# A hybrid trunk step on one core: gated branch products kept in their banks, and the mixed chunk rounded by ScalarE

## What is computed

```python
br = jnp.stack([a_out, b_out, c_out, d_out], axis=2)
gates = jax.nn.sigmoid(gpre.reshape(B, S, N_BRANCH, D_MODEL))
mixed = jnp.sum(gates * jnp.einsum('bsnc,ncd->bsnd', br, p['w_branch']), axis=2)
x = x + gate1 * (mixed @ p['w_out'])
h2 = rms_norm(x, p['norm2_w']) * (1 + scale2) + shift2
x = x + gate2 * expert_choice_ffn(h2, p['w_router'], p['w_gate'], p['w_up'], p['w_down'])
```

## Time and profile before

| | |
|---|---|
| median of three runs | 2066.54 us |
| profiled execution | 2068.15 us (span of its trace 2066.4 us) |
| PE busy | 1793.6 us, 87% |
| DVE busy | 645.3 us, 31% |
| ACT busy | 548.3 us, 27% |
| POOL busy | 518.7 us, 25% |
| mean granted clock of TensorE | 0.95 |
| chain that ended last | PE 49%, DMA 33%, DVE 9%, POOL 4%, ACT 3% |

### The profile page before, as it was taken

How to read it: one execution, slowest core, us unless ns; L and a number is a source line. 1 busy time by engine, 2 the same in 40 slices (tenths; PEclk the granted TensorE clock), 3 DMA queues, 4 the chain that set the end, 5 groups by cost and what they waited for, 6 DMA issues and landing times.

```text
span 2066.4 us, 22539 instructions
## 1 busy us (share of the span) xinstructions
PE 1793.6 (87%) x9096; PEld 1138.6 (55%) x9096; DVE 645.3 (31%) x1349; ACT 548.3 (27%) x1054; POOL 518.7 (25%) x654
## 2 busy tenths in 40 slices
PE   5989999999899788878879899999996987888787
PEld 2878897789553222222248788967882422222223
DVE  2185245647310001001144642556653000000111
ACT  3433343222431111101144333522224211110111
POOL 0785343148200000000037652523561000000000
PEclk8999898999999999999989998989998999999999
DMA  9524533455589999999973253335544999999996
GB/s 350 138 102 138 181 105 117 175 165 207 207 360 426 426 427 426 428 426 427 427 210 123 79 206 111 113 138 172 194 177 170 389 427 428 426 428 426 427 426 265
DMA packets 123543, 567.76 MB, mean 275 GB/s; under 512 B 21808, under 2 KB 31280, under 8 KB 98352
## 3 DMA queue, kind: packets, MB, share of 16 engines
q1 hardware_dynamic: 112656, 543.91, 66.5%
q10 hardware_dynamic: 9920, 20.84, 2.8%
q0 software_dynamic: 864, 1.58, 0.3%
HBM read 550.57 MB, written 15.73 MB: 274 GB/s over the span
## 4 chain that ended last, share of the span: by engine, by line
PE 49%; DMA 33%; DVE 9%; POOL 4%; ACT 3%; issue 1%; SPq 1%; ACTq 0%; DVEq 0%
PE banks L769 22%; PE banks L1269 11%; DMA ring<-in_w_up 9%; DMA ring<-in_w_gate 7%; DMA ring<-in_w_down 6%; DMA work<-in_w_gate 4%; POOL ring_fp32r L710 3%; DMA work<-in_w_up 3%; PE banks L775 2%; DMA ring<-in_w_ada 2%; DVE work L1845 2%; DMA work<-in_w_down 1%; PE banks L1086 1%; PE banks L1065 1%; ACT work L1368 1%; PE banks L1239 1%
## 5 line engine op out<-in xcount | busy, mean ns | idle before, releaser
L710 POOL TENSOR_TENSOR ring_fp32r<-ring,ring_fp32r 128x256 fp32r<-128x256 f32 x592 | 467.2, 822 | 912.4 <-ACT ring_fp32r L1368 911.9
L1269 PE MATMUL banks<-ring,work 128*64 128x512 f32 x1776 | 402.6, 597 | 74.9 <-DMA ring<-in_w_gate 33.3
L769 PE MATMUL banks<-xT_fp32r,ring_fp32r 128*128 128x384 f32 x1280 | 356.0, 351 | 1.6 <-POOL ring_fp32r L710 1.6
L1368 ACT ACTIVATE work<-banks 32x512 f32<-32x512 f32 (+7 forms) x404 | 205.7, 528 | 487.3 <-PE banks L1269 250.8
L1269 PEld LDWEIGHTS banks<-ring,work 128*64 128x64 f32 x1776 | 122.4, 136 | 333.2 <-issue 198.8
L1269 PE MATMUL banks<-work 128*64 128x512 f32 x972 | 225.8, 601 | 42.8 <-DMA work<-in_w_gate 15.1
L769 PEld LDWEIGHTS banks<-xT_fp32r,ring_fp32r 128*128 128x128 f32 x1280 | 241.3, 195 | 10.6 <-issue 3.6
L769 PE MATMUL banks<-hT_fp32r,ring_fp32r 128*128 128x384 f32 x640 | 219.4, 343 | 0.0
L1368 ACT ACTIVATE ring_fp32r<-ring 128x1024 fp32r<-128x1024 f32 (+1 forms) x164 | 154.8, 970 | 158.2 <-PE banks L769 126.8
L2247 DVE SCALAR_TENSOR_TENSOR xT<-banks,mod,xT 128x128 f32<-128x128 f32 (+1 forms) x128 | 47.0, 413 | 446.3 <-PE banks L1305 446.0
L1269 PEld LDWEIGHTS banks<-work 128*64 128x64 f32 x972 | 67.7, 137 | 182.9 <-issue 112.4
(11 more groups left out here) (287 smaller groups left out, 1687.3 us busy)
## 6 DMA issues: line engine op xcount, KB each, us to landing
ring<-in_w_up SPq DMA_DIRECT2D x38, 2048.0 KB, 30.6
ring<-in_w_gate SPq DMA_DIRECT2D x37, 2048.0 KB, 30.5
ring<-in_w_down SPq DMA_DIRECT2D x36, 2048.0 KB, 30.3
ring<-in_w_in SPq DMA_DIRECT2D x28, 2048.0 KB, 8.4
ring<-in_w_ada SPq DMA_DIRECT2D x24, 2048.0 KB, 8.5
work<-in_w_down SPq DMA_DIRECT2D x20, 2048.0 KB, 30.6
work<-in_w_gate SPq DMA_DIRECT2D x18, 2048.0 KB, 30.5
work<-in_w_up SPq DMA_DIRECT2D x16, 2048.0 KB, 30.6
```

The lines of the kernel that those rows point to most:

```text
L710: ins = pool.tensor_tensor(rounded(w_), w_, rounded(hi_), ALU.subtract)
L769: mm = pe.matmul(dst, a_, b_, start=(first and i == 0), stop=(last and i == 2))
L1269: mm = pe.matmul(dst[64 * hf:64 * hf + 64, :], x(k), w[kk][:, 512 * hf:512 * hf + 512], start=(k == 0), stop=(k == KC - 1), tile_position= ...
L1368: return act.activation(dst, src, ACT.Copy, scale=scale)
```

## The change

In VectorE's loop the products of banks b and b + 1 are written back into these banks (one instruction of 768 columns); those of banks b + 2 and b + 3 go to TMPB. Three sums of 384 columns follow, each with one operand in a bank and one in TMPB: bank b plus TMPB 0 into bank b; bank b + 1 plus TMPB 1 into TMPB 1; bank b plus TMPB 1 into MIX. The last of them counts up `bp_evac`, so the banks are released at the end of a chunk and not after its products. The cast leaves VectorE.

ScalarE gets a loop over the eight chunks: it rounds weight quarter `Q_BRANCH + dc + 4`, waits for `bp_evac` of chunk dc, writes the rounded chunk MIXH, counts up `mix_ready`, and for the first four chunks issues the gate load of chunk dc + 4. GpSimd's, TensorE's and SP's code is the same.

```diff
--- before.py
+++ after.py
@@ -1608,17 +1608,18 @@
 
                 for slot in spilled:
                     act.wait_ge(slot, 16 * (SPILLED // 8) * (l + 1))
-                for dc in range(8):
+                for dc in range(4):
                     if dc == 0:
                         act.wait_ge(sem["br_ready"], l + 1)
                     if dc == 2:
                         act.wait_ge(sem["tokens_free"], l + 1)
-                    if dc >= 4:
-                        high_parts(Q_BRANCH + dc + 1)
-                        act.wait_ge(sem["mix_ready"], 8 * l + dc - 3)
                     act.dma_start(GT[dc % 4], spill[l, dc]).then_inc(gate_in[dc % 4], 16)
-                for dc in range(4, 8):
+                for dc in range(8):
                     high_parts(Q_BRANCH + dc + 5)
+                    act.wait_ge(sem["bp_evac"], 8 * l + dc + 1)
+                    copy(rounded(MIXH[:, dc, :]), MIX[:, dc, :]).then_inc(sem["mix_ready"], 1)
+                    if dc < 4:
+                        act.dma_start(GT[dc], spill[l, dc + 4]).then_inc(gate_in[dc], 16)
                 for k in range(KC):
                     if k < 4:
                         high_parts(Q_OUT + k + 5)
@@ -2187,15 +2188,15 @@
                     dve.wait_ge(sem["bp_out"], 8 * l + dc + 1)
                     dve.wait_ge(gate_in[dc % 4], 16 * (2 * l + dc // 4 + 1))
                     b = 4 * (dc % 2)
-                    STT(TMPB[:, 0:3, :], GT[dc % 4], 1.0, PS[:, b:b + 3, 0:T], ALU.add, ALU.mult)
-                    STT(TMPB[:, 3, :], GATES[:, dc, :], 1.0, PS[:, b + 3, 0:T], ALU.add, ALU.mult).then_inc(sem["bp_evac"], 1)
+                    STT(PS[:, b:b + 2, 0:T], GT[dc % 4][:, 0:2, :], 1.0, PS[:, b:b + 2, 0:T], ALU.add, ALU.mult)
+                    STT(TMPB[:, 0, :], GT[dc % 4][:, 2, :], 1.0, PS[:, b + 2, 0:T], ALU.add, ALU.mult)
+                    STT(TMPB[:, 1, :], GATES[:, dc, :], 1.0, PS[:, b + 3, 0:T], ALU.add, ALU.mult).then_inc(dve_step, 1)
+                    dve.wait_ge(dve_step, step())
+                    TTo(PS[:, b, 0:T], PS[:, b, 0:T], TMPB[:, 0, :], ALU.add)
+                    TTo(TMPB[:, 1, :], PS[:, b + 1, 0:T], TMPB[:, 1, :], ALU.add).then_inc(dve_step, 1)
+                    dve.wait_ge(dve_step, step())
+                    TTo(MIX[:, dc, :], PS[:, b, 0:T], TMPB[:, 1, :], ALU.add).then_inc(sem["bp_evac"], 1)
                     dve.wait_ge(sem["bp_evac"], 8 * l + dc + 1)
-                    TTo(TMPB[:, 0:2, :], TMPB[:, 0:2, :], TMPB[:, 2:4, :], ALU.add).then_inc(dve_step, 1)
-                    dve.wait_ge(dve_step, step())
-                    TTo(MIX[:, dc, :], TMPB[:, 0, :], TMPB[:, 1, :], ALU.add).then_inc(dve_step, 1)
-                    dve.wait_ge(dve_step, step())
-                    dve.tensor_copy(rounded(MIXH[:, dc, :]), MIX[:, dc, :]).then_inc(sem["mix_ready"], 1)
-                    dve.wait_ge(sem["mix_ready"], 8 * l + dc + 1)
                 for dc in range(8):
                     if dc == 0:
                         dve.wait_ge(sem["x_moved"], 32 * (l + 1))
```

## The result

The changed kernel took 2047.42 us (median of 7 runs, 2039.8 to 2053.39), the kernel before, run beside it, 2058.64 us (7 runs). The ratio is 0.9933, 95% interval 0.9907 to 0.9959: faster by 0.67%. The interval reaches past 0.995, so whether the gain is over the half percent that the prediction set as its bound isn't decided. Over all repeated runs of this study the two means are 2061.4 us (66 runs of before) and 2049.4 us (25 of after), 12.1 us apart with a standard error of 1.2. The forecast was 8.6 us less and 2057.9 us, with a range down to 2048.0. The result is 0.6 us under that range.

The account below looks back on a forecast made before the run. VectorE and GpSimd, taking turns in the branch sums, were held to share the bound. TensorE's lost times there, 4.3 us a layer, gave 2 x 4.3 = 8.6 us off the median 2066.54: 2057.9 us, range 2048 to 2067.

Parts of the forecast that it names:

- The bound: In the branch sums of each layer: GpSimd carries the chain at 4.97 us a round, VectorE is as full.
- GpSimd's piece of 0.72 us: One 128x256 weight subtraction on GpSimd (L710): 0.72 us without turns with VectorE, against 1.54 beside an SBUF-to-SBUF sum.
- TensorE without a stop: Branch matmuls and first 48 of the output projection in one group, no wait on VectorE or GpSimd: 4.3 us a layer.
- The break-even for a late release: In the branch sums: banks freed at chunk end; at 4.8 us a VectorE chunk the output projection starts as before.
- A: VectorE's bank writes cost double: 4.75 us a chunk, gain 0.4 to 0.6 us a layer, about 2065.5; chance 0.10.
- C: Slower: banks come free late in the branch sums; at 5.6 us a chunk 11 us lost, about 2078; chance 0.05.
- B: GpSimd's pieces don't get faster: 5.0 us a chunk, TensorE resumes at 508 as before, 2066.5; chance 0.08.
- D: Layer 1's gain is swallowed by the expert weight stream; one layer's 4.3 us remains, 2062.2; chance 0.07.
- the start of the sum: The level for the whole program: median of before, 2066.54 us, from three runs spanning 2056.85 to 2066.82.
- the later stages wait on this chain, so I pass the gain on in full: Stages behind the branch sums in both layers start earlier by the whole gain, 2 x 4.3 = 8.6 us.
- The term of the sum: Gain from the first branch matmul to the output projection's first pair: 4.3 us a layer, 8.6 us in all.
- 0.62 for the same: Whole program: chance of a time within half a percent, 10.3 us (2056.2 to 2076.9), of the kernel before.

Follow-up runs that it names:

- the control: The changed kernel with one more 128x384 product on VectorE a chunk, one operand in a bank; first branch matmul to pair's end 45.01 and 45.26 us.

## Why the prediction was right or wrong

**Right.** The bound: GpSimd and VectorE share it and slow each other (the kernel with only the cast moved, the extra subtraction, and the two added products). VectorE's chunk of 3.54 us: measured 3.54. The bank-to-bank product of 951 ns: 963; the sum in its bank of 545: 566. GpSimd's piece of 0.72 us: 0.738 in the median, with gaps. TensorE without a stop: one group, 4.46 and 4.62 us gained for 4.3. The break-even for a late release, at VectorE's time a chunk c = 4.8: 50.1 us measured where the formula gives 49.8 at 4.95. But that nothing waits as long as c is under 4.22 is too strong: at c = 4.00 the control lost 1 us a layer. Moved behind ScalarE's wait, the weight rounding and gate loads cost nothing.

**Rivals.** A and C fall by the price of a bank write, 963 and 566 ns. B falls by 738 ns a piece. D falls too: in layer 1, from 469 matmuls behind the pair to the last one, it takes 417.7 to 418.1 us in the traces of before and 418.0 to 418.1 after, so the gain ahead of it is passed on whole.

**Wrong: the level and the range.** The step that failed first is the start of the sum, "from the median: 2057.9 us": it is the largest part of the error. I built the time on the median of three runs, 2066.54. Over 66 runs before has a mean of 2061.4 and spans 2047.5 to 2070.5; the three happened to hold two of its slow half. That put the forecast 5.1 us too high. The gain of 12.1 us for 8.6 is 3.5 more, and the last 2 us are luck of the series: its median, 2047.42, lies under the changed kernel's mean of 2049.4. The lower end, 2048.0, was the quickest of three runs less 8.6 us, so it had no room for these. From the 2058.64 us that before took beside the changed kernel, the same 8.6 us give 2050.0, inside the range.

**Wrong: the sum.** The second step that failed is "the later stages wait on this chain, so I pass the gain on in full", which puts what the later stages do at nothing. The chain is passed on, but TensorE's granted clock in a later stage isn't the same when that stage comes at another time: 3.5 us more were gained behind layer 0's pair, 0.6 lost behind layer 1's and 3.6 lost in layer 1's mixers. The term of the sum came out at 9.0 for 8.6. In the traces the others nearly cancel, so of the 3 us by which all runs exceed the stretches the cause stays open.

**The chances.** With 8.6 us against a bound of 10.3 a further 2 us of anything tips it. The measured intervals, 0.9907 to 0.9959 first, leave open on which side of half a percent the kernel lies, so 0.62 for the same isn't refuted.

**Wrong: what the cast is worth.** The prediction counted the cast among what leaves VectorE and didn't price the sums without it. The sums alone shorten the stretch as much.

## What to carry to other kernels

When two engines are both full in a stretch and single instructions of one get longer beside certain instructions of the other, an edit on one can relieve both: look for instructions with two SBUF operands on VectorE beside GpSimd work, and give one operand a bank. A release that moves to the end of a chunk was free at 3.54 us a chunk against the producer's 4.22, cost about 1 us a layer at 4.00, and all that had been won at 4.8. And a few microseconds gained ahead of a stage in which TensorE starts and stops may come out larger or smaller, by where its clock is down there: price the stretch, and keep some 4 us either way for the stages behind it. Three runs that spread over 10 us don't give a level; take more, or forecast the difference.

## What the runs showed of the hardware

- An fp32 sum of 384 columns takes 545 to 566 ns with a bank operand, whether it writes a bank or SBUF. A product of 384 columns with both operands in SBUF takes 551 ns when it begins ahead of GpSimd's subtraction, which then takes 1.05 us in place of 0.74, and up to 1047 ns when the subtraction began first. Beside the sums of the kernel before a GpSimd piece took up to 1.54 us. The Trainium skill, "SBUF — State Buffer", section "Who interferes with whom", has this rule of two SBUF inputs, and the pair of added products agrees.
- VectorE writes a bank from the same bank at nearly the price of an SBUF output: 768 columns in 963 ns, where the estimate from SBUF outputs was 951, and a sum of 384 in 566 ns against 548.
- What the low TensorE clock costs a stage reproduced from run to run of one kernel behind layer 0's pair (four traces of four, three of three), at the change of layers only in three of four, and it changed with small edits far ahead. The same 16 matmuls took 5.35 or 3.65 us by it.
